# Down projection with five seven-product sets in every pair of column blocks, and weights loaded in half places

## The chip, the cores and the metric

The kernel runs on one core of a Trainium2 chip. The time is the device time of one execution in microseconds, the median of the runs. Five engines work side by side and meet only at semaphores: TensorE (PE) multiplies, VectorE (DVE) and ScalarE (ACT) work elementwise, GpSimd (POOL) here mostly issues accumulating DMAs, SyncE (SP) issues the loads.

## The reference

Two layers over 256 tokens of 2048 features. Layer 0 mixes by causal pooling, layer 1 by windowed attention; each is followed by a gated feed-forward part of 5632 columns. A change in the last product of that part is what this case is about:

```python
D_MODEL = 2048; SEQ = 256; DEPTH = 2
D_FF = ((8 * D_MODEL // 3 + 255) // 256) * 256          # 5632

def swiglu(x, wg, wu, wd):
    return (jax.nn.silu(x @ wg) * (x @ wu)) @ wd

for layer in range(DEPTH):
    ...                                                  # pooling mixer, or K/V, Q and attention
    h = h + swiglu(rmsnorm(h, ffn_norm[layer]), w_gate[layer], w_up[layer], w_down[layer])
return rmsnorm(h, final_norm)
```

All of it is float32, and the output is the whole (1, 256, 2048) array.

## The kernel before

**Precision.** Every float32 factor is split in two parts that TensorE can take in its faster format: `w_hi` is a rounded copy of the weights, made by ScalarE, and `w_lo` what is left, made by VectorE as `raw - w_hi`. A product is then three matmuls of 128 by 128 by 512: hi by hi, hi by `w_lo`, lo by hi.

**Units.** Weights pass through a ring of four places (`RING = 4`). A unit is 128 x 1024 weights, two tiles of 128 rows by 512 columns. For unit n ScalarE waits until TensorE has used unit n-4 and until the raw weights have landed, and rounds (L924 in the down projection, `L690` with a gain in K/V and Q); VectorE subtracts (L1538; L1129 in K/V and Q) and raises `unit_ready`; TensorE multiplies and raises `unit_used`. All three walk the same list of units in order, and everything else that ScalarE and VectorE do is hung behind a unit of that list.

**The down projection** of a layer (`down(l)` on each engine, planned by `DownPlan`) multiplies the 256 x 5632 matrix hT with w_down, 44 row tiles by four column blocks of 512. Blocks are done in two pairs (0 and 1, then 2 and 3). An **own** unit is two row tiles of one block for both token tiles: 12 matmuls. A **set** replaces eight own half products by seven: four row tiles of both blocks of a pair are taken as a 2 x 2 matrix B11, B12, B21, B22 of 256 x 512 each and multiplied with sums of quarters of hT in seven units B11, B21, B22, T1, T2, T3, T4 of 6 matmuls each. Four row tiles of a pair thus cost 42 matmuls in 7 units as a set and 48 in 4 units as own. The order is written out by hand in `DOWN_ORDER`, one character a unit: 0 and 1 are own units of the pair's first and second block, a, b, c are B11, B21, B22, and t, u, v, w are T1 to T4. `DOWN_SETS = [(4, 3), (4, 4)]` says how many sets the pairs of layer 0 and of layer 1 have: 15 in all, 109 units in layer 0 and 112 in layer 1.

**The sums of a set.** T1 is B11 with B12 added, T2 is T1 with B22 added, T4 is B21 with T2 added, T3 is B22 with B12 added (signs are carried by the other factor). Before, a set has two whole places of 1024 KB, loaded from column blocks one and two. GpSimd adds B12 to B11 by an SBUF-to-SBUF accumulating DMA (L2235, waited for as `d1_in`), waits for it, and adds B22 onto B12 in the same way (L2237, `d3_in`). T2 and T4 are added by VectorE (L1546, L1550) behind fixed units. The other factor's sums, "rows", are made per set by VectorE (`down_sums`, L1474 to L1482, and L1486) and ScalarE (L946).

**Loads.** SyncE issues 44 loads of 1024 KB a layer (L630), each when the unit that used its place last has been split.

**Around the matmuls.** At the start of `down` the last turn of the gate and up products is still being finished: `gate_add`, `sum_silu`, `up_add`, `common_out`, two whole transposes of 128 x 512 on VectorE (`quad_turn`, L1294) and, on ScalarE, sixteen copies of 32 x 256 (`quad_move`, L729) that put the 32 x 32 blocks in their places. When a pair's last set is done, `pair_common` adds the shared sums into h; when a block's last unit is done, `down_out` adds the block's products (L1216). In layer 0, blocks 0 to 2 of h are then transposed for the K/V and Q products that follow, on VectorE, as 16 transposes of 32 x 256 per block that write straight into place (`h_turn`, L1192, in four steps of four), rounded by ScalarE (`x_hi_part`, L714) and subtracted by VectorE (`x_lo_part`, L1199). Block 3 is transposed by TensorE inside K/V. ScalarE also sums squares of each block (L761). In the last four units of layer 1 TensorE does token tile 0 first and then tile 1 in two halves, so that the final norm can start (`finish`).

The positions of these steps come from formulas and small lists (`SET_AT`, `UP_AT`, `QUAD_AT`, `LAST_AT`, `down_turn`, `out_after`).

Of the kernel before, what the change touches and what calls it, by code (L numbers as in the profile page):

```python
# [26 lines left out]
F32 = mybir.dt.float32  # L27
# [5 lines left out]
P = 128  # L33
# [79 lines left out]
class TurnsPlan:  # L113

    def __init__(self):
# [8 lines left out]
        self.count = [0] * HALVES  # L124
# [15 lines left out]
FIRST_SLOT = ("B11", "B21", "T1", "T2", "T4")  # L140
HALF = {"B11": 0, "B21": 2 * C, "T1": 0, "T2": 0, "T3": 0, "T4": 2 * C, "B22": 2 * C}
DOWN_SETS = [(4, 3), (4, 4)]


DOWN_ORDER = [('a000b00t000acu1wb1tvcubwav11001100cat0ucb0wtvuvw11111111',
               '00a0000bc00taubvc0t01u1vwba1cw001tu1wv000101111111111'),
              ('0a01b1t00uwvca0001b0c01t0avuc1wbt111uw110ac0b00t1vuwv111',
               'b00a00act0b0utwvbacuw0v000001a1btcuwc1t1uvwv101011111111')]


@dataclass
class Load:

    slot: int
    block: int
    k0: int
    nth: int
    ready: int
    first: int
# [3 lines left out]
class Unit:  # L163
# [6 lines left out]
    load: Load  # L170
    second: object
    off: int
# [4 lines left out]
class DownPlan:  # L177

    def __init__(self, sets, order):
        self.units, self.loads = [], []  # L180
# [16 lines left out]
        needs = {}  # L197
        for n, (pair, form, n_set, m, k) in enumerate(where):
            if form == "own":
                needs.setdefault((pair, "own", m, k // 4 * 4), []).append(n)  # L200
                continue
            if form in FIRST_SLOT:
                needs.setdefault((pair, "sum", 0, 4 * n_set), []).append(n)
            if form not in ("B11", "B21", "T4"):
                needs.setdefault((pair, "sum", 1, 4 * n_set), []).append(n)
        self.free = [max(TURNS.free[2 * i:2 * i + 2]) - SUM_STEPS for i in range(SLOTS)]
        rows_used = max(AT[u] for u in SUM_ORDER if u[0] in PARTS) + 1
        self.free[RING] = max(self.free[RING], rows_used + RING - SUM_UNITS)
        count = [0] * SLOTS
        loads = {}  # L210
        for key in sorted(needs, key=lambda key: (needs[key][0], key[2])):
            pair, kind, m, k = key
            slot = min(range(SLOTS), key=lambda one: (self.free[one], one))
            count[slot] += 1
            loads[key] = Load(slot, 2 * pair + m, k, count[slot], self.free[slot], needs[key][0])
            self.loads.append(loads[key])
            self.free[slot] = max(needs[key]) + 1
        self.loads.sort(key=lambda one: (one.ready, one.first, one.slot))
        self.count = count

        self.sums = {}
        for pair, form, n_set in sorted((one for one in self.at if one[1] == "T1"), key=self.at.get):
            n = self.at[pair, form, n_set]
            self.sums.setdefault(n, []).append((pair, "T2", n_set))
            self.sums.setdefault(min(n + 1, self.at[pair, "T4", n_set] - 1), []).append((pair, "T4", n_set))
        self.nth_sum = {one: n for n, one in enumerate(one for n in sorted(self.sums) for one in self.sums[n])}
        self.set_order = sorted((one[::2] for one in self.at if one[1] == "B11"),
                                key=lambda one: self.at[one[0], "B11", one[1]])
# [13 lines left out]
        for n, (pair, form, n_set, m, k) in enumerate(where):  # L242
            if form == "own":
                load, second, off = loads[pair, "own", m, k // 4 * 4], None, k % 4 * C
            else:
                off = HALF[form]
                load = loads[pair, "sum", 0 if form in FIRST_SLOT else 1, 4 * n_set]
                second = loads[pair, "sum", 1, 4 * n_set]
            self.units.append(Unit(pair, form, n_set, m, k, load, second, off,
                                   tuple(opened[d] == n for d in banks[n]), tuple(closed[d] == n for d in banks[n])))  # L250

DOWN = [DownPlan(DOWN_SETS[l], DOWN_ORDER[l]) for l in range(2)]
# [3 lines left out]
class Lap:  # L256
# [17 lines left out]
    def loads(self, slot):  # L274
        more = -2 * SUM_TURNS * self.layers + (DOWN[0].count[slot] - 4 * UF // 8) * self.downs
        return self.n + more
# [39 lines left out]
def trunk(nc, x, pool_w, pool_rows, pool_scale, w_kv, w_q, w_o, w_gate, w_up, w_down, final_norm,  # L316
# [6 lines left out]
    down_v = [rows(w_down[l]) for l in range(2)]  # L323
# [5 lines left out]
    with ExitStack() as ctx:  # L329
# [38 lines left out]
        last_quad = [at(f"last_quad{l}", [P, T, C], F32, o_xhi + 4 * (0, 12)[l] * S) for l in range(2)]  # L368
        def d_home(l, n):
            tile = D_TILE[l][n]  # L370
            return (o_s1hi, o_s1lo) if tile is None else (o_xhi + 4 * tile * S, o_xlo + 4 * tile * S)
# [67 lines left out]
        raw_in = [sem(f"raw_in{i}") for i in range(RING + 1)]  # L439
        half_in = [sem(f"half_in{i}") for i in range(HALVES)]  # L440
# [99 lines left out]
        def out_after(l, b):  # L540
            plan = DOWN[l]
# [1784 lines left out]
```

## Time and profile before

| | |
|---|---|
| median of 3 runs | 1644.01 us (1641.56 to 1646.27) |
| profiled execution | 1647.76 us, span of its trace 1646.0 us |
| PE busy | 1630.0 us, 99% of the span |
| VectorE, ScalarE, GpSimd busy | 1441.4, 1196.3, 162.9 us |
| down projection, layer 0 | 494.9 to 724.9 us |
| down projection, layer 1 | about 1405 to 1639 us, the final norm behind it |
| granted TensorE clock | 0.999 of full speed |

A table of stretches gives, for each engine, its busy time and the number of its instructions in the stretch, then the granted clock and the busy share of the DMA engines. A timeline row gives the start, the length, engine, line, operation, what is written and read, how many instructions are merged, and in brackets how long the engine stood idle before it and what ended that. The length of an instruction in a row can overlap the next one's start: in a dense stretch the distance between starts is what an instruction costs. Times are us from the start of the span.

### The profile page before, as it was taken

The numbers are of one execution on the slowest core, as the hardware profiler recorded it, in microseconds if no ns is written. First come the engines' busy times: TensorE is split into PE (matmuls) and PEld (weight loads), VectorE is DVE, ScalarE is ACT, GpSimd is POOL, SyncE is SP. The second block draws the span as 40 slices with busy tenths as digits, with TensorE's granted clock in tenths as the row PEclk, the third lists the DMA queues.
The fourth block names the chain that finished last, engine by engine and source line by source line (L and its number), as shares of the span: only waits on it lengthen the run. The fifth ranks groups of instructions, "written<-read, shape, count | busy, mean of one in ns | idle before, by whom it ended". The sixth has DMA issues, their size and how long they took to land.

```text
span 1646.0 us, 20218 instructions
## 1 busy us (share of the span) xinstructions
PE 1630.0 (99%) x7396; PEld 1339.1 (81%) x7396; DVE 1441.4 (88%) x1622; ACT 1196.3 (73%) x1720; POOL 162.9 (10%) x204
## 2 busy tenths in 40 slices
PE   9999999999999999999999999999999999999998
PEld 8888888888888888888777888888887888788887
DVE  6899999999999898777676869999999999888867
ACT  6688888888867755556665567888888887676653
POOL 1111111111100000002010001111111111000000
PEclk9999999999999999999999999999999999999999
DMA  8578888888888887855444556888888888887783
GB/s 297 187 187 251 243 246 244 246 244 245 245 225 232 236 269 211 262 179 191 142 130 153 183 215 160 236 241 242 242 247 241 237 243 233 279 236 248 217 260 143
DMA packets 136571, 368.98 MB, mean 224 GB/s; under 512 B 9876, under 2 KB 10004, under 8 KB 136344
## 3 DMA queue, kind: packets, MB, share of 16 engines
q1 hardware_dynamic: 114576, 298.46, 51.1%
q0 software_dynamic: 21600, 68.17, 23.0%
q8 instruction: 59, 0.97, 0.2%
q10 hardware_dynamic: 296, 1.06, 0.2%
q14 instruction: 40, 0.33, 0.1%
HBM read 349.82 MB, written 2.10 MB: 214 GB/s over the span
## 4 chain that ended last, share of the span: by engine, by line
PE 82%; DMA 8%; DVE 6%; ACT 2%; issue 1%; SPq 0%; ACTq 0%; POOLq 0%
PE acc L1926 7%; PE acc L1928 7%; PE acc L1927 7%; PE acc L1775 6%; PE acc L1776 6%; PE acc L1777 6%; PE acc L2018 5%; PE acc L2020 5%; PE acc L2019 5%; DMA raw<-w_up_in 5%; PE acc L1903 5%; PE acc L1905 5%; PE acc L1907 5%; PE acc L2003 3%; PE acc L2004 3%; PE acc L2005 3%
## 5 line engine op out<-in xcount | busy, mean ns | idle before, releaser
L843 ACT ACTIVATE w_hi<-raw 128x1024 fp32r<-128x1024 f32 (+1 forms) x500 | 490.2, 1005 | 109.6 <-PE acc L1907 53.8
L1375 DVE TENSOR_TENSOR w_lo<-raw,w_hi 128x1024 fp32r<-128x1024 f32 (+1 forms) x460 | 507.4, 1149 | 17.0 <-ACT w_hi L843 14.9
L924 ACT ACTIVATE w_hi<-raw 128x1024 fp32r<-128x1024 f32 x221 | 232.8, 1060 | 160.3 <-PE acc L2020 112.6
L1538 DVE TENSOR_TENSOR w_lo<-raw,w_hi 128x1024 fp32r<-128x1024 f32 x221 | 265.9, 1222 | 62.4 <-ACT w_hi L924 57.3
L2224 POOL DMA_DIRECT2D raw<-w_up_in x120 | 104.6, 872 | 833.7 <-DVE w_lo L1372 504.5
L1903 PE MATMUL acc<-w_hi,xT_hi 128*128 128x512 f32 x480 | 186.8, 389 | 0.0
L1905 PE MATMUL acc<-w_lo,xT_hi 128*128 128x512 f32 x480 | 186.8, 389 | 0.0
L1907 PE MATMUL acc<-w_hi,xT_lo 128*128 128x512 f32 x480 | 186.7, 389 | 0.0
L2018 PE MATMUL acc<-w_hi,hT_hi 128*128 128x512 f32 x456 | 177.7, 390 | 1.6 <-DVE w_lo L1538 1.3
L2020 PE MATMUL acc<-w_hi,hT_lo 128*128 128x512 f32 x456 | 177.4, 389 | 0.0
L2019 PE MATMUL acc<-w_lo,hT_hi 128*128 128x512 f32 x456 | 177.4, 389 | 0.0
L729 ACT ACTIVATE hT_f<-quad 32x256 f32<-32x256 f32 x320 | 132.8, 415 | 4.5
L1926 PE MATMUL acc<-w_hi,s_hi 128*128 128x512 f32 x320 | 125.9, 393 | 3.2 <-DVE w_lo L1375 3.1
L1928 PE MATMUL acc<-w_hi,s_lo 128*128 128x512 f32 x320 | 124.7, 390 | 0.0
L1927 PE MATMUL acc<-w_lo,s_hi 128*128 128x512 f32 x320 | 124.6, 389 | 0.0
L1124 DVE TENSOR_TENSOR w_lo<-raw,w_hi 128x1024 fp32r<-128x1024 f32 x72 | 88.2, 1236 | 31.9 <-ACT w_hi L687 31.6
L687 ACT ACTIVATE w_hi<-raw 128x1024 fp32r<-128x1024 f32 x72 | 75.5, 1063 | 54.3 <-PE acc L1777 48.9
L1775 PE MATMUL acc<-w_hi,xT_hi 128*128 128x512 f32 x288 | 114.2, 397 | 0.0
L1777 PE MATMUL acc<-w_hi,xT_lo 128*128 128x512 f32 x288 | 112.2, 390 | 0.0
L1776 PE MATMUL acc<-w_lo,xT_hi 128*128 128x512 f32 x288 | 112.1, 389 | 0.0
L1926 PE MATMUL acc<-w_hi,xT_hi 128*128 128x512 f32 x280 | 109.0, 389 | 0.0
L1928 PE MATMUL acc<-w_hi,xT_lo 128*128 128x512 f32 x280 | 109.0, 389 | 0.0
(222 smaller groups left out, 3087.2 us busy)
## 6 DMA issues: line engine op xcount, KB each, us to landing
raw<-w_down_in SPq DMA_DIRECT2D x88, 1024.0 KB, 6.7
raw<-w_gate_in SPq DMA_DIRECT2D x160, 512.0 KB, 6.1
raw<-w_up_in SPq DMA_DIRECT2D x100, 512.0 KB, 6.1
raw<-w_up_in POOLq DMA_DIRECT2D x80, 512.0 KB, 7.5
raw<-w_q_in SPq DMA_DIRECT2D x16, 1024.0 KB, 5.1
raw<-w_o_in SPq DMA_DIRECT2D x16, 1024.0 KB, 5.1
raw<-raw POOLq DMA_DIRECT2D x30, 512.0 KB, 5.9
raw<-w_up_in POOLq DMA_DIRECT2D x40, 256.0 KB, 5.5
```

What stands on the lines that cost most here:

```text
L843: nc.scalar.activation(w_hi[:, (before + n) % RING, 0:src.shape[-1]], src, ACT.Copy, scale=-1.0 if form == "B11" else 1.0).then_inc(hi_rea ...
L1375: nc.vector.tensor_tensor(lo, src, hi, ALU.subtract).then_inc(unit_ready, 1)
L1538: nc.vector.tensor_tensor(w_lo[:, LAP_DOWN[l].ring(n), :], src, w_hi[:, LAP_DOWN[l].ring(n), :].bitcast(F32), ALU.subtract).then_inc(unit_ ...
L1903: nc.tensor.matmul(dst, xT_hi[:, k, tok], w_hi[:, w, cols], start=start, stop=False, skip_group_check=True)
L1905: nc.tensor.matmul(dst, xT_hi[:, k, tok], w_lo[:, w, cols], start=False, stop=False, skip_group_check=True)
L1907: last = nc.tensor.matmul(dst, xT_lo[:, k, tok], w_hi[:, w, cols], start=False, stop=stop, skip_group_check=True)
L1926: nc.tensor.matmul(dst, x_hi, w_hi[:, w, cols], start=start, stop=False, skip_group_check=True)
L1927: nc.tensor.matmul(dst, x_hi, w_lo[:, w, cols], start=False, stop=False, skip_group_check=True)
L1928: last = nc.tensor.matmul(dst, x_lo, w_hi[:, w, cols], start=False, stop=stop, skip_group_check=True)
L2018: nc.tensor.matmul(dst, hT_hi[:, k, tok], w_hi[:, LAP_DOWN[l].ring(n), cols], start=start, stop=False)
L2019: nc.tensor.matmul(dst, hT_hi[:, k, tok], w_lo[:, LAP_DOWN[l].ring(n), cols], start=False, stop=False)
L2020: last = nc.tensor.matmul(dst, hT_lo[:, k, tok], w_hi[:, LAP_DOWN[l].ring(n), cols], start=False, stop=stop)
```

## The change

1. `DOWN_SETS` becomes `[(5, 5), (5, 5)]`: 20 sets, 118 units in each layer, with new orders. All four pairs now have 24 own units and 35 of sets.
2. Weights are loaded in half places of 512 KB, one unit each (78 loads a layer), from a w_down that is laid out by blocks outside the kernel, so that a partition's part is one run of 4 KB and not four of 2 KB. B12 is no longer loaded: GpSimd adds it twice from DRAM, onto B11 (T1) and, after the T2 sum, onto B22 (T3). These 20 DMAs a layer go by `accums`, sorted by place, with at most four under way (`DOWN_LANES`).
3. In layer 0, h is transposed by two whole 128 x 512 transposes per block on VectorE into `h_quad`, and ScalarE moves the blocks by 16 copies of 32 x 256 per block (`h_move`).
4. Every step beside the matmuls gets a place of its own in `DOWN_AT`.
5. In `pair_common` VectorE waits for ScalarE's copy before its first add and not after it.

```diff
-DOWN_SETS = [(4, 3), (4, 4)]
+DOWN_SETS = [(5, 5), (5, 5)]
-DOWN_ORDER = [('a000b00t000acu1wb1tvcubwav11001100cat0ucb0wtvuvw11111111',
-               '00a0000bc00taubvc0t01u1vwba1cw001tu1wv000101111111111'),
...
+DOWN_ORDER = [('baab000101c01b10c1t0auw1tav10t1wa1vcub01ct0tcwbvuuvuwwv1001',
+               'aa0cbaa011ttbcuwcatwcuuvt1vtc0bv0vu0uv10b1w1bww010000101111'),
+              ('ba0b01001a100at10cwu10at1cvuca1tw10ut1vcut0cbvuvwb1bwvw0101',
+               'aaa000c0bctccw1au0t1ut0vbawb1v0wut0ct1buv10wvbuwv1101001111')]
+DOWN_AT = [{...
+     "copy": (57, 109), "common": (57, 108), "out": (61, 61, 115), "squares": (87, 105, 117),
+     "h_turn": ((98, 102), (97, 100), (115, 115)),
+     "h_moves": ((103, 105, 108, 110, 110, 113, 113, 114), (102, 108, 108, 111, 111, 113, 113, 115), (117, 117, 117, 117, 117, 117, 117, 117)),
+     "x_hi": (115, 117, 117), "x_lo": (117, 117, 117)},
...
+            def h_move(b, n):
+
+                if n == 0:
+                    ac.wait_ge(h_turned, T * (b + 1))
+                pb = n // 2
+                for q in (2 * (n % 2), 2 * (n % 2) + 1):
+                    src = h_quad[b][pb * QUAD:(pb + 1) * QUAD, :, :].rearrange("c t (k q r) -> c k t q r", k=4, q=4)
+                    dst = xT_f[q * QUAD:(q + 1) * QUAD, 4 * b:4 * b + 4, :].rearrange(
+                        "c k (t b r) -> c k t b r", t=T, b=4)
+                    last = nc.scalar.activation(dst[:, :, :, pb, :], src[:, :, :, q, :], ACT.Copy)
+                if n == 7:
+                    last.then_inc(xt_full, 1)
...
+                    if form == "own":
+                        src = down_v[l][2 * pair + m, k // 2]
+                    else:
+                        src = down_v[l][2 * pair + (form == "B22"), 2 * m + (form != "B11")]
+                    sp.dma_start(down_half(one), src.rearrange("p k n -> p (k n)")).then_inc(half_in[one.half], 16)
...
-                    gp.dma_start(first[:, 0:2 * C], second[:, 0:2 * C], accum_op=ALU.add).then_inc(d1_in, 16)
-                    gp.wait_ge(d1_in, 16 * (c + 1))
-                    gp.dma_start(second[:, 0:2 * C], second[:, 2 * C:], accum_op=ALU.add).then_inc(d3_in[c % 2], 16)
+                    base = {"T1": "B11", "T3": "B22"}[form]
+                    gp.wait_ge(unit_ready, before + plan.at[pair, base, n_set] + 1)
+                    if form == "T3":
+                        gp.wait_ge(d_sum, down_sum(l, (pair, "T2", n_set)))
+                    if c >= DOWN_LANES:
+                        gp.wait_ge(*lane(c - DOWN_LANES))
+                    b12 = down_v[l][2 * pair + 1, 2 * n_set].rearrange("p k n -> p (k n)")
+                    gp.dma_start(set_half(l, pair, base, n_set), b12, accum_op=ALU.add).then_inc(lane(c)[0], 16)
```

Two places as the engines' programs show them. First, ScalarE at the end of layer 0's down projection and the start of K/V, before. `w_hi` from `raw` is the rounding of a unit (the last four are own units), `unused,sumsq<-h` the squares of block 2, `xT_hi<-xT_f` the rounding of its transposed block, `w_hi<-raw,gains` half of a K/V unit.

```order
L761 ACTIVATE unused_113,sumsq_119<-h_49 128x2x2x128 [waits sq_done,job_out,pair_step]
L761 ACTIVATE unused_113,sumsq_119<-h_49 128x2x2x128 [waits sq_done]
L924 ACTIVATE w_hi_60<-raw_59 128x1024 [waits unit_used]
L924 ACTIVATE w_hi_60<-raw_59 128x1024 [waits raw_in0,unit_used]
L924 ACTIVATE w_hi_60<-raw_59 128x1024 [waits unit_used]
L924 ACTIVATE w_hi_60<-raw_59 128x1024 [waits raw_in2,unit_used]
L714 ACTIVATE xT_hi_56<-xT_f_58 128x1024 [waits xt_full]
L924 ACTIVATE w_hi_60<-raw_59 128x1024 [waits unit_used]
L690 ACTIVATE w_hi_60<-raw_59,gains_115 128x512 [waits unit_used,raw_in0]
L690 ACTIVATE w_hi_60<-raw_59,gains_115 128x512
```

And the same place after, where `h_quad2` is the transposed block 2:

```order
L929 ACTIVATE w_hi_60<-raw_59 128x1024 [waits half_in2,unit_used]
L929 ACTIVATE w_hi_60<-raw_59 128x1024 [waits half_in6,unit_used]
L772 ACTIVATE unused_124,sumsq_130<-h_49 128x2x2x128 [waits sq_done,job_out,pair_step]
L772 ACTIVATE unused_124,sumsq_130<-h_49 128x2x2x128 [waits sq_done]
L712 ACTIVATE xT_hi_56<-xT_f_58 128x1024 [waits xt_full]
L740 ACTIVATE xT_f_58<-h_quad2_82 32x8x32 [waits h_turned]
L740 ACTIVATE xT_f_58<-h_quad2_82 32x8x32 x15
L712 ACTIVATE xT_hi_56<-xT_f_58 128x1024 [waits xt_full]
L688 ACTIVATE w_hi_60<-raw_59,gains_126 128x512 [waits unit_used,raw_in0]
L688 ACTIVATE w_hi_60<-raw_59,gains_126 128x512
```

The squares of block 2 stood five units before the end; now they, two roundings of transposed blocks and all sixteen moves of block 2 stand between the rounding of the last down unit and that of the first K/V unit.

Second, VectorE at the same place, before: the last steps of `h_turn` for block 2, three splits, the subtraction, and the first K/V split.

```order
L1192 STREAM_TRANSPOSE xT_f<-h 32x2x4x32 x4
L1538 TENSOR_TENSOR w_lo<-raw,w_hi 128x1024 [waits hi_ready]
L1192 STREAM_TRANSPOSE xT_f<-h 32x2x4x32 x4
L1538 TENSOR_TENSOR w_lo<-raw,w_hi 128x1024 [waits hi_ready] x3
L1199 TENSOR_TENSOR xT_lo<-xT_f,xT_hi 128x1024 [waits xt_hi]
L1129 SCALAR_TENSOR_TENSOR w_lo<-raw,gains,w_hi 128x512 [waits hi_ready]
```

And after, from `down_out` of block 2 on:

```order
L1228 SCALAR_TENSOR_TENSOR h<-acc,r,h 128x512 [waits unit_used,pair_step]
L1228 SCALAR_TENSOR_TENSOR h<-acc,r,h 128x512
L1596 STREAM_TRANSPOSE h_quad_82<-h 128x512 [waits unit_used,pair_step,job_out]
L1596 STREAM_TRANSPOSE h_quad_82<-h 128x512
L1549 TENSOR_TENSOR w_lo<-raw,w_hi 128x1024 [waits hi_ready] x2
L1211 TENSOR_TENSOR xT_lo<-xT_f,xT_hi 128x1024 [waits xt_hi] x3
L1141 SCALAR_TENSOR_TENSOR w_lo<-raw,gains,w_hi 128x512 [waits hi_ready]
```

`down_out` of block 2 stood behind unit 101 of 0 to 108; now it stands behind unit 115 of 0 to 117, and three subtractions of transposed blocks stand ahead of the first K/V split.

## Rows read from the trace of the kernel before

**Rows 1.** Stretches of both down projections: us; PE, PEld, DVE, ACT, POOL busy; clock; DMA

```profile
494.90:724.90 230.00, 229.74 (x1012) 189.48 (x1011) 202.95 (x224) 143.55 (x169) 12.15 (x14) 1.00 0.75 230
1404.60:1632.20 227.60, 225.91 (x995) 186.03 (x994) 187.02 (x179) 142.22 (x166) 13.90 (x16) 1.00 0.77 232
```

**Rows 2.** TensorE's waits: who waited, for whom, us in total, times, longest

```profile
PE acc L1810 <- DVE hT_lo L1136: 1.8, 1, 1.8
...
PE acc L2018 <- DVE w_lo L1538: 1.3, 2, 1.1
```

**Rows 3.** Timeline of TensorE, layer 0: an own unit, then a set's unit (first matmuls)

```profile
576.75 0.39 PE L2018 MATMUL acc<-w_hi,hT_hi 128*128 128x512 f32 x1
...
579.47 0.39 PE L2003 MATMUL acc<-w_hi,hT_hi 128*128 128x512 f32 x1
...
580.83 0.39 PE L2003 MATMUL acc<-w_hi,d_hi 128*128 128x512 f32 x1
```

**Rows 4.** Groups on VectorE, layer 0's down projection: busy us, mean ns | idle before

```profile
L1538 DVE TENSOR_TENSOR w_lo<-raw,w_hi 128x1024 fp32r<-128x1024 f32 x108 | 129.8, 1222 | 22.2 <-ACT w_hi L924 19.4
L1192 DVE STREAM_TRANSPOSE xT_f<-h 32x256 f32<-32x256 f32 x48 | 20.9, 436 | 0.8
L1546 DVE TENSOR_TENSOR raw<-raw 128x1024 f32<-128x1024 f32 x7 | 8.5, 1219 | 0.0
```

**Rows 5.** The same table for ScalarE: the copies that move turned blocks

```profile
L729 ACT ACTIVATE hT_f<-last_quad 32x256 f32<-32x256 f32 x16 | 6.6, 415 | 0.3
```

**Rows 6.** Timeline of VectorE: a split, a whole transpose, a split; and a `down_out`

```profile
504.28 1.22 DVE L1538 TENSOR_TENSOR w_lo<-raw,w_hi 128x1024 fp32r<-128x1024 f32 x1
505.42 0.70 DVE L1294 STREAM_TRANSPOSE last_quad<-act 128x512 f32<-128x512 f32 x1
506.04 1.18 DVE L1538 TENSOR_TENSOR w_lo<-raw,w_hi 128x1024 fp32r<-128x1024 f32 x1
...
1619.18 1.40 DVE L1216 SCALAR_TENSOR_TENSOR h<-acc,r,h 128x512 f32<-128x512 f32 x2
```

**Rows 7.** Timeline of ScalarE: two copies, and the squares of one block

```profile
508.42 0.85 ACT L729 ACTIVATE hT_f<-quad 32x256 f32<-32x256 f32 x2
...
702.53 0.61 ACT L761 ACTIVATE unused<-h 128x512 f32<-128x512 f32 x1
...
703.26 0.63 ACT L761 ACTIVATE unused<-h 128x512 f32<-128x512 f32 x1
```

**Rows 8.** Timeline of ScalarE where layer 0's down projection ends

```profile
713.41 1.04 ACT L714 ACTIVATE xT_hi<-xT_f 128x1024 fp32r<-128x1024 f32 x1
715.16 1.06 ACT L924 ACTIVATE w_hi<-raw 128x1024 fp32r<-128x1024 f32 x1 [0.71 <-PE acc L2020]
719.15 2.79 ACT L690 ACTIVATE w_hi<-raw,gains 128x512 fp32r<-128x512 f32 x4 [2.93 <-DMA raw<-w_kv_in]
```

**Rows 9.** Timeline of VectorE at the same place: the first two K/V units

```profile
720.52 2.87 DVE L1129 SCALAR_TENSOR_TENSOR w_lo<-raw,gains,w_hi 128x512 fp32r<-128x512 f32 x4 [1.91 <-ACT w_hi L690]
```

**Rows 10.** The chain in order of time, where layer 1's down projection waits

```profile
1410.86 8.01 DMA raw<-raw
...
1424.20 0.50 PE acc L2018
...
1543.18 8.37 DMA raw<-w_down_in
```

**Rows 11.** DMA issues of the whole run: count, KB each, median us to landing

```profile
raw<-w_down_in SPq DMA_DIRECT2D x88, 1024.0 KB, 6.7
...
raw<-w_up_in SPq DMA_DIRECT2D x100, 512.0 KB, 6.1
raw<-w_up_in POOLq DMA_DIRECT2D x80, 512.0 KB, 7.5
```

**Rows 12.** From issue to landing of the 512 KB loads of L624: least, median, most

```profile
DMA to landing us min/median/max: 2.5/6.2/11.1
```

**Rows 13.** A stretch around TensorE's longest wait, columns as in the first group

```profile
24.00:32.00 8.00, 6.24 (x35) 5.19 (x34) 7.53 (x12) 5.48 (x10) 2.05 (x2) 1.00 0.81 295
```

**Rows 14.** Timeline of VectorE at the end: the wait for the last matmuls

```profile
1639.01 0.48 DVE L1731 SCALAR_TENSOR_TENSOR hblk<-acc,r,hblk 128x256 f32<-128x256 f32 x1 [0.89 <-PE acc L2177]
```

More of the change, by code:

```diff
@@ L169 @@
     k0: int
-    load: Load
-    second: object
-    off: int
+    piece: Piece
     opens: tuple
@@ L218, in __init__ @@
[L218 to L226, printed above, removed]
@@ L227, in __init__ @@
-        self.set_order = sorted((one[::2] for one in self.at if one[1] == "B11"),
-                                key=lambda one: self.at[one[0], "B11", one[1]])
+        self.sums = {}
+        for pair in range(2):
+            for m in range(sets[pair]):
+                n = self.at[pair, "T1", m]
+                self.sums.setdefault(n, []).append((pair, "T2", m))
+                n = max(min(n + 1, self.at[pair, "T4", m] - 1), self.at[pair, "B21", m])
+                self.sums.setdefault(n, []).append((pair, "T4", m))
@@ new lines, in __init__, with at @@
+        self.nth_sum = {one: n for n, one in enumerate(one for n in sorted(self.sums) for one in self.sums[n])}
+        sum_at = {one: n for n in self.sums for one in self.sums[n]}
+        life = {}
+        for n, (pair, form, m, block, k) in enumerate(where):
+            if form == "own":
+                life[pair, "own", block, k] = (n, n)
+        for pair in range(2):
+            for m in range(sets[pair]):
+                def at(form):
+                    return self.at[pair, form, m]
+                life[pair, "B11", m, 0] = (at("B11"), max(at("T2"), sum_at[pair, "T4", m] + 1))
+                life[pair, "B21", m, 0] = (at("B21"), at("T4"))
+                life[pair, "B22", m, 0] = (min(at("B22"), sum_at[pair, "T2", m]), at("T3"))
@@ L229, in __init__ @@
+        self.pieces.sort(key=lambda one: (one[0].ready, one[0].first, one[0].half))
+        self.accums = sorted([(self.at[p, "B11", m], 0, "T1", p, m) for p in range(2) for m in range(sets[p])]
+                             + [(max(self.at[p, "B22", m], sum_at[p, "T2", m]), 1, "T3", p, m)
+                                for p in range(2) for m in range(sets[p])])
+        self.nth_accum = {one[2:]: c for c, one in enumerate(self.accums)}
         opened, closed = {}, {}
@@ L242, in __init__ @@
         for n, (pair, form, n_set, m, k) in enumerate(where):
[L243 to L249, printed above, removed]
+            piece = self.of[pair, "own", m, k] if form == "own" else self.of[pair, PLACE[form], n_set, 0]
+            self.units.append(Unit(pair, form, n_set, m, k, piece,
                                    tuple(opened[d] == n for d in banks[n]), tuple(closed[d] == n for d in banks[n])))
+DOWN_LANES = 4
 DOWN = [DownPlan(DOWN_SETS[l], DOWN_ORDER[l]) for l in range(2)]
@@ L322, in trunk @@
     up_v = [w_up[l] for l in range(2)]
-    down_v = [rows(w_down[l]) for l in range(2)]
+    down_v = [w_down[l] for l in range(2)]
     kv_v, q_v, o_v = rows(w_kv), rows(w_q[0]), rows(w_o[0])
@@ L1587, in _ @@
+                    if l == 1:
+                        for b, when in enumerate(at["gain"]):
+                            if n == when:
+                                ve.wait_ge(pair_step, 8 * (2 + b // 2 + 1))
+                                final_gain(b)
             gate_up(0, 0, True)
```

282 lines of the change are left out of this document (129 added, 153 removed).

## The prediction

> **What bounds the kernel now.** I read the busy times by stretch first, then who waited for whom, then timelines. In both down projections TensorE is busy for all but 0.26 us and 1.69 us, at the full granted clock [rows 1], and over the whole run its listed waits are a few tenths to 1.8 us [rows 2]. The bound is the number of matmuls, so the first question is what a matmul costs: not the 0.39 us of its row, since rows overlap, but the distance between starts. An own unit of 12 matmuls runs from 576.75 to 579.47, that is 2.72 us or 0.227 us a matmul; a set's unit of six takes 1.36 us [rows 3]. The second question is whether the feeders keep up. VectorE is busy 203 of 230 us in layer 0's down projection and 187 of 227.6 us in layer 1's, ScalarE some 143 us in each [rows 1]. In a dense stretch a split costs VectorE 1.14 us (504.28 to 505.42) [rows 6], against 1.36 us for a set's unit on TensorE: only 0.22 us is over, and the ring is four units deep.
>
> **Matmuls removed.** A set saves 6 matmuls. Layer 0 goes from 7 sets to 10, layer 1 from 8 to 10: 18 + 12 = 30 matmuls. TensorE's programs differ by just that, so this step can't fail to happen. 30 x 0.227 = **-6.8 us** (4.1 and 2.7), on the engine that sets the end.
>
> **Splits and sums added.** Layer 0 gets 9 more units, 6 more T2 or T4 sums and one more set of rows. By [rows 4] that is 9 x 1.22 + 6 x 1.22 on VectorE, and for the rows some 4.1 us (two instructions of 1.22 and four of 0.42); the 48 small transposes (20.9 us) become six whole ones of 0.70 [rows 4, 6], 16.7 us less. VectorE goes from 203 to 209 of about 226 us. Layer 1 gets 6 units, 4 sums and a set of rows: 187 + 16.3 = 203 of 226 us. This all lies beside TensorE as long as no stretch asks more of VectorE than four units of lead can lend. I summed, place by place, VectorE's steps against TensorE's units in the new order: a set's unit lends 0.22 us, an own unit 1.58, a sum takes 1.14. The lead that a unit's split has on TensorE is then 0.4 us at the least (layer 0, unit 37, behind rows and a sum), mostly 0.7 to 3. So the cost is 0; if that cover is gone at the tightest places, some tenths each. ScalarE: 24 pairs of moves of 0.85 [rows 7] in layer 0, with 9 roundings: about 143 + 31 = 174 of 226 us. Room on the whole; where it is at the end is the next term.
>
> **The end of layer 0's down projection.** Here is what I expect to go wrong. Before, the last block's ten own units cover all the turning of block 2: its rounding is over at 714.4, the first K/V unit is rounded from 719.15, when its load lands, and TensorE does not wait [rows 8, 9]. After, block 2's last unit is 113, and only units 114 to 117 remain: 4 x 2.72 = 10.9 us of cover. Time from the end of unit 113: semaphore 0.3; `down_out` on VectorE 1.4 [rows 6], to 1.7; the squares on ScalarE 2 x 0.73 [rows 7], to 3.2; rounding block 1, 1.0 (1.04 in its row [rows 8]), to 4.2; sixteen moves at 0.425 [rows 5, 7], 6.8, to 11.0; rounding block 2, 1.0, to 12.0; the first K/V unit's rounding, two of four in 2.79, so 1.4 [rows 8], to 13.4; its split, two of four in 2.87 [rows 9], to 14.8. VectorE's two transposes end by 3.0 and bind nothing. TensorE runs out at 10.9: **+3.9 us** of wait, with nothing else for it to do, since it walks the list in order. Bounds: 3.4 if every step is at its row's distance with no semaphore delay, 4.5 with 0.1 us at each of the six handovers. Behind ScalarE's moves K/V's roundings are queued, behind VectorE's subtraction of block 2 K/V's splits; units 2 on have their lead back, since 1.4 us per unit is fed and 2.7 used. K/V's loads, now released by units 115 to 117, land inside this wait.
>
> **Waits that go.** Layer 1 waits 1.1 us at 1424.20, behind an SBUF-to-SBUF accumulate of 8.01 us [rows 10] whose B11 stood only five units ahead. In the new orders B11 stands at least 15 us ahead of its T1, and T2 and B22 at least 12 us ahead of T3; the slowest comparable accumulate, DRAM to SBUF, has a median of 7.5 us [rows 11]. So that wait goes: **-1.1**. Also -0.3, the wait behind the 8.37 us load at 1543 [rows 10], and -0.2 in layer 0, where the small transposes crowd VectorE. The 0.3 us of "issue" I leave.
>
> **Loads.** Bytes fall: a set moves 2.5 MB and not 3. What counts is the time between a place's release and its next use. Six places are close. Tightest: layer 1's unit 76, released by unit 72: TensorE's units 72 to 75 take 6.8 us, the split of 72 leads by 0.9, and rounding and split of 76 take 2.4: 5.3 us for a load whose like has a median of 6.2 and ranges from 2.5 to 11.1 [rows 12]. **+0.9**, bounds 0 and 5.8. Next: layer 0's unit 30 (6.4 us), 79 (7.3), layer 1's 86, 87, 89 (7.3, 7.4, 7.8): 0 at the median. Before, the tightest were 8.0 and 8.1 for 1024 KB loads of 6.7 [rows 11], and one gave the 0.3 us.
>
> What rows show of size: 512 KB loads land in 6.1 us, 1024 KB in 6.7 [rows 11], so halves land sooner but not in half the time. The Trainium skill's "DMA: Bandwidth & Descriptors", section "Measured (HBM→SBUF, 128 partitions, SWDGE, issued from GpSimd)", speaks against the change: batch DMAs to 1 MiB or more for at least 75% of peak. By that rule the halves would be slow and the late-load case below the likely one; by the rows, the sum stands.
>
> **The end of the kernel.** Before, the second tile's last part waits 0.89 us for TensorE [rows 14]. After, block 2's add, two splits, and two gains stand in the last four units. The split of unit 116 is ready 0.2 us after TensorE wants it: **+0.2**. `finish` of tile 0 starts 0.6 us later than it could, inside the 0.89. The changed order of copy and add in `pair_common` has 8 us of own units above it: 0.
>
> **Sum.** -6.8 + 3.9 - 1.6 + 0.9 + 0.2 = **-3.4 us**. The profiled execution took 1647.76 us, 3.75 above the median: it would become 1644.4. The median becomes 1644.0 - 3.4 = **1640.6 us**. A measurement of this kernel tells about 0.3%, 4.9 us, from no change.
>
> **Rivals.**
> 1. The end of layer 0 is covered after all, say because moves beside an idle list run closer: 3.9 falls away, **1636.7**. For: the steps are many and I sum them singly. Against: each is a row, and ScalarE does them in order. 0.12.
> 2. VectorE does not keep up. At 92% busy, ten sums of 20 stand within a set-heavy run; 0.3 us at each of ten places is 3.0: **1643.6**. For: before, it waited only 22.2 us for roundings in that stretch [rows 4]. Against: the summed lead never falls below 0.4. 0.13.
> 3. Slower: late loads. If the halves land in 8.4 us, like the load in [rows 10], the six places above miss by 2.0 + 1.1 + 3.1 + 1.1 + 1.0 + 0.6 = 8.9 us, 8.0 more than I count: **1648.6**. From 7.5 us of landing on it eats the gain (3.8 - 0.9 = 2.9). For: the accumulates from DRAM now come by 20 a layer with up to four under way. Against: fewer bytes. 0.13.
> 4. The wait breaks TensorE's clock. Rows show waits up to 1.8 us with the clock still at the higher of its levels, 2.4 GHz, in the stretch around [rows 2, 13]; 3.9 us is not shown. At 1.2 GHz a matmul takes 0.227 us more. For as long as the wait itself, that is 1.9 us, **1642.5**; for all 96 matmuls of K/V 21.8 us, 1662.4. It outweighs the gain from 15 matmuls on. 0.10, of which a quarter beyond 1649.
>
> The Trainium skill's "TensorE: Matmul & The Clock Gate", section "What's actually happening", says that the throttled state is the default and activity releases it. By that, rival 4 would hold; no row here has a wait that long, so it stays a rival.
>
> **How the numbers follow.** Forecast 0.50, rivals 0.12, 0.13, 0.13, 0.10, other 0.02. The likeliest case alone: 1638.5 to 1642.5. The range of 1636.5 to 1647.5 takes in rivals 1 and 2 and most of 4, and half of 3. Faster by over 0.3% is below 1639.1: rival 1 and a quarter of the forecast (a run's spread), 0.25. Slower, above 1648.9: a little under half of 3, a quarter of 4 and the rest, 0.10. Within: 0.65.
>
> **What would show it.** Right: 996 matmuls in each down projection; one TensorE wait of 3.4 to 4.5 us at the first K/V unit, ended by VectorE's split and behind sixteen copies on ScalarE; no wait of T1 or T3 for an accumulate; about 1 us at unit 76 of layer 1 behind a load. VectorE at 209 and 203 us. Wrong: no wait at K/V, many waits of tenths in sets, a granted clock below full behind the K/V wait, or loads that land above 7.5 us.

## The result, and the profile after

| | before | after |
|---|---|---|
| median of 22 runs each | 1642.95 us (1640.48 to 1646.38) | 1645.95 us (1642.71 to 1648.13) |
| ratio to before | | 1.0019, 95% interval 1.0013 to 1.0025 |
| profiled execution, span | 1647.76 us, 1646.0 us | 1647.64 us, 1645.9 us |
| PE busy | 1630.0 us | 1625.7 us |

The changed kernel is slower by 0.19%, about 3.0 us, where I forecast 3.4 us less. The time lies inside the range and inside "within 0.3%"; the sign is wrong, and the sum is short by 6.4 us. (I forecast from a median of 3 runs, 1644.01 us; that of 22 is 1642.95, so the differences are what can be compared.) TensorE's busy time fell by 4.3 us, although some of its matmuls became slower: the gain was made and then given back, mostly as waits.

The two profiled executions happen to take the same time: that of before is 4.8 us above its median, that of after 1.7. Their totals can't be subtracted, so I compare stages. The first table of waits is TensorE's in the changed kernel (for whom, us in total, times, longest) and answers to [rows 2]:

```profile
PE acc L2037 <- DVE w_lo L1549: 4.2, 3, 2.8
PE acc L1794 <- DVE w_lo L1141: 3.8, 1, 3.8
PE acc L1829 <- DVE hT_lo L1148: 1.7, 1, 1.7
```

The K/V wait of 3.8 us is the one forecast. The 2.8 us in a down projection is new. The stages, from the starts of TensorE's first matmul in each (its timeline, in us from the span's start; in brackets the length of the stage):

| kernel | layer 0 down | K/V | layer 1 down | last matmul |
|---|---|---|---|---|
| before | 495.08 | 725.84 (230.76) | 1407.83 (681.99) | 1638.69 (230.86) |
| after | 495.92 | 731.47 (235.55) | 1411.24 (679.77) | 1638.90 (227.66) |

Layer 1 gained 3.2 us; layer 0 lost 4.8, and 1.8 more at the start of K/V. The stretch between, which the change touches only by those 1.8 us at its start, is 2.2 us shorter all the same. Over all profiles below it ranges from 678.2 to 683.0, well beyond those 1.8 us, so a difference of some two us in it is the spread of an execution.

TensorE's timeline in the changed kernel, at the two waits (start, length, line, in brackets the idle time before):

```profile
556.89 0.39 PE L2024 MATMUL acc<-w_hi,d_lo 128*128 128x512 f32 x1
560.04 0.50 PE L2037 MATMUL acc<-w_hi,hT_hi 128*128 128x512 f32 x1 [2.76 <-DVE w_lo L1549]
...
561.43 0.63 PE L2038 MATMUL acc<-w_lo,hT_hi 128*128 128x512 f32 x1
561.86 0.63 PE L2039 MATMUL acc<-w_hi,hT_lo 128*128 128x512 f32 x1
...
564.26 0.40 PE L2039 MATMUL acc<-w_hi,hT_lo 128*128 128x512 f32 x1
...
731.47 0.77 PE L1794 MATMUL acc<-w_hi,xT_hi 128*128 128x512 f32 x1 [3.78 <-DVE w_lo L1141]
...
734.89 0.40 PE L1796 MATMUL acc<-w_hi,xT_lo 128*128 128x512 f32 x1
```

Read the distances. After the wait a matmul starts 0.43 us after the one before it (561.43, 561.86), not 0.227 as in [rows 3]. From 560.04 to 564.26 eleven steps take 4.22 us and would take 2.49 at full speed: 1.73 us lost on top of the wait. At K/V the eight steps from 731.47 to 734.89 take 3.42 us for 1.81, which is 1.6 lost. A wait also delays the next start by 0.16 us more than its idle time in the row, since the last matmul's length overlaps; with that K/V's price behind its wait is 1.77. The stretches say why; columns as in [rows 1], with the granted clock third from the end:

```profile
555.00:560.00 5.00, 2.28 (x11) 1.54 (x9) 1.24 (x2) 2.28 (x4) 0.00 (x0) 1.00 0.49 193
560.00:564.00 4.00, 3.96 (x11) 3.12 (x12) 4.00 (x4) 3.38 (x5) 0.21 (x1) 0.58 0.61 157
564.00:568.00 4.00, 4.00 (x19) 3.30 (x18) 3.71 (x4) 2.68 (x3) 0.66 (x1) 0.99 0.82 187
...
731.00:735.00 4.00, 3.54 (x9) 2.85 (x10) 4.00 (x7) 2.55 (x5) 0.00 (x0) 0.57 0.28 46
```

The clock was granted at 0.58 and 0.57 in the four microseconds after each wait, most of which thus lie at the lower of its levels (1.2 GHz), and behind unit 30 it is back at 0.99, the higher one (2.4 GHz). So both waits cost about 1.8 us more than they last.

What ended the first? The chain in order of time, then ScalarE's timeline, then the DMA issues of 543 to 549 us (count, KB, median us to landing), all of the changed kernel:

```profile
548.47 9.12 DMA raw<-w_down_in
557.67 1.07 ACT w_hi L929
558.76 1.24 DVE w_lo L1549
560.04 0.50 PE acc L2037
```

```profile
557.67 1.06 ACT L929 ACTIVATE w_hi<-raw 128x1024 fp32r<-128x1024 f32 x1 [4.61 <-DMA raw<-w_down_in]
```

```profile
raw<-w_down_in POOLq DMA_DIRECT2D x2, 512.0 KB, 8.2
raw<-w_down_in SPq DMA_DIRECT2D x1, 512.0 KB, 9.1
```

This is layer 0's unit 30, one of the six places whose budget I had worked out (6.4 us), and its load took 9.1. After it landed came only its rounding (1.07 us) and its split (1.24), so nothing else held the unit back. GpSimd had started two accumulates just before it:

```profile
545.68 1.76 POOL L2256 DMA_DIRECT2D raw<-w_down_in  x2 [6.74 <-issue]
```

One more wait in layer 0 was not forecast: 0.86 us at 694.75, unit 106, with 0.1 to 0.2 us of slower matmuls behind it. In layer 1 there is one of 0.62 at 1574.33, unit 87, behind a load of 8.0 us.

### The profile page after: what moved, and what is told of

Same layout as the page of the kernel before. It is cut to its first block, busy times and chain, and to the rows that moved or that the text cites. A ratio compares the mean times of both kernels' runs of the same rounds, so it can differ in the third digit from the quotient of the medians.

```text
span 1645.9 us, 20453 instructions
## 1 busy us (share of the span) xinstructions
PE 1625.7 (99%) x7366; PEld 1336.3 (81%) x7366; DVE 1457.8 (89%) x1617; ACT 1233.2 (75%) x1785; POOL 171.6 (10%) x214
## 4 chain that ended last, share of the span: by engine, by line
PE 88%; DMA 4%; DVE 4%; ACT 2%; issue 1%; SPq 0%; ACTq 0%; POOLq 0%; DVEq 0%
PE acc L1945 8%; PE acc L1947 8%; PE acc L1946 8%; PE acc L1794 6%; PE acc L1922 6%; PE acc L1926 6%; PE acc L1924 6%; PE acc L1796 6%; PE acc L1795 6%; PE acc L2037 5%; PE acc L2039 5%; PE acc L2038 5%; PE acc L2023 3%; PE acc L2022 3%; PE acc L2024 3%; DMA raw<-w_up_in 2%
## 5 line engine op out<-in xcount | busy, mean ns | idle before, releaser
L929 ACT ACTIVATE w_hi<-raw 128x1024 fp32r<-128x1024 f32 x236 | 248.2, 1060 | 138.1 <-PE acc L2039 87.9
L1549 DVE TENSOR_TENSOR w_lo<-raw,w_hi 128x1024 fp32r<-128x1024 f32 x236 | 282.0, 1219 | 42.4 <-ACT w_hi L929 37.4
L2037 PE MATMUL acc<-w_hi,hT_hi 128*128 128x512 f32 x376 | 147.5, 392 | 4.2 <-DVE w_lo L1549 4.2
L2039 PE MATMUL acc<-w_hi,hT_lo 128*128 128x512 f32 x376 | 147.0, 391 | 0.0
L2038 PE MATMUL acc<-w_lo,hT_hi 128*128 128x512 f32 x376 | 146.9, 391 | 0.0
L1136 DVE TENSOR_TENSOR w_lo<-raw,w_hi 128x1024 fp32r<-128x1024 f32 x72 | 88.1, 1235 | 31.9 <-ACT w_hi L685 31.6
L685 ACT ACTIVATE w_hi<-raw 128x1024 fp32r<-128x1024 f32 x72 | 75.5, 1063 | 54.3 <-PE acc L1796 49.0
```

The lines of the kernel that those rows point to most:

```text
L929: nc.scalar.activation(w_hi[:, LAP_DOWN[l].ring(n), :], down_half(unit.piece), ACT.Copy).then_inc(hi_ready, 1)
L1549: nc.vector.tensor_tensor(w_lo[:, LAP_DOWN[l].ring(n), :], down_half(unit.piece), w_hi[:, LAP_DOWN[l].ring(n), :].bitcast(F32), ALU.subtra ...
L2037: nc.tensor.matmul(dst, hT_hi[:, k, tok], w_hi[:, LAP_DOWN[l].ring(n), cols], start=start, stop=False)
L2039: last = nc.tensor.matmul(dst, hT_lo[:, k, tok], w_hi[:, LAP_DOWN[l].ring(n), cols], start=False, stop=stop)
```

## The experiments

The theory: the gain from the matmuls, 6.8 us, is there in full; it is paid away by two waits on TensorE, each with a fall of the granted clock. Wait one is a load that shares the DMA engines with accumulates, wait two ScalarE's queue at the end of layer 0. Rivals: that load is slow by itself; the end is bound by another engine or by loads once ScalarE is relieved; the slow matmuls have a cause other than TensorE's idleness.

**The accumulate moved.** `down_turn_sums`, on GpSimd; set 3's B12 is needed at unit 41 and was added after unit 25:

```
+ late = 31 if (l, form, pair, n_set) == (0, "T1", 0, 3) else 0
- gp.wait_ge(unit_ready, before + plan.at[pair, base, n_set] + 1)
+ gp.wait_ge(unit_ready, before + max(plan.at[pair, base, n_set] + 1, late))
```

> The changed kernel with one edit: in layer 0 GpSimd starts the first accumulate of set 3 (pair 0) after the split of unit 30 instead of after that of unit 25; it is needed at unit 41. In the profile of the changed kernel this accumulate and another one started at 546.6 and 545.7 us, and the load for unit 30 that was issued at 548.5 us between them landed after 9.1 us against a budget of 6.4. Theory A (the load was late because it shared the DMA engines with two accumulates): the load lands within 7.5 us, the wait of 2.76 us at unit 30 is under 0.8, no matmul stretch there at 0.43 us spacing (those cost 1.73 us), and the time falls by 3 to 4.5 us against the changed kernel (ratio to the kernel before 1.0019 -> 0.9993 to 1.0001). Theory B (this load is slow by itself, or the wait happened in that one execution only): the landing stays at 8 to 9 us and the wait stays, or the time stays within 0.5 us of the changed kernel's.

Measured: 1643.26 us, ratio 0.9999 (0.9988 to 1.0009). GpSimd's timeline shows the second accumulate gone from beside the first, and the DMA issues of 544 to 548.5 us show what that does for the loads:

```profile
544.96 0.86 POOL L2257 DMA_DIRECT2D raw<-w_down_in  x1 [6.74 <-issue]
555.08 0.86 POOL L2257 DMA_DIRECT2D raw<-w_down_in  x1 [9.25 <-DVE w_lo L1549]
```

```profile
raw<-w_down_in POOLq DMA_DIRECT2D x1, 512.0 KB, 5.5
raw<-w_down_in SPq DMA_DIRECT2D x1, 512.0 KB, 4.0
```

Landing fell from 9.1 to 4.0 us, the wait at unit 30 is gone, no matmul near it stands at 0.43 us, and layer 0's stage is 231.70 instead of 235.55 us. Theory A holds. In the three kernels below that also keep the two accumulates together, the waits there were 1.92, 2.09 and 2.23 us, behind loads of 8.3, 8.4 and 8.6 us: it is a property of the kernel and not of one execution.

**K/V's first units ahead of block 2.** ScalarE's loop over the K/V units (VectorE's subtraction of block 2 follows its unit 3 likewise):

```
- for b in range(NBLK - 1):          # in down(0): h_moves, x_hi
+ for b in range(NBLK - 2):
...
  round_hi(LAP_KV, i, tiles, off, G_KV, k0)
+ if i in (1, 2):
+     for part in range(4 * i - 4, 4 * i):
+         h_move(2, part)
+ if i == 3:
+     x_hi_part(0, 2)
```

> The changed kernel with one edit at the end of layer 0: ScalarE rounds the first two K/V weight units before the 16 moves of block 2, the third between them and the fourth before block 2 is rounded; VectorE rounds block 2 after the fourth unit. TensorE needs block 2 only from the fifth K/V unit on. Theory A (the 3.78 us wait is ScalarE's 6.81 us of moves standing ahead of the first K/V unit in its queue, and the clock then costs 1.77 us more): no wait over 0.3 us at the start of K/V, none over 0.5 us at the fifth unit, full-speed spacing of 0.227 us throughout, time 5 to 5.5 us below the changed kernel's (ratio to before about 0.9987). Theory B (VectorE's chain or the K/V loads would come next): a wait of 1 to 3 us remains at the start or at the fifth unit, and the gain is under 3 us.

Measured: 1640.31 us, ratio 0.9985 (0.9975 to 0.9995). ScalarE's timeline, where K/V now starts at 724.97 without a wait:

```profile
718.19 1.32 ACT L688 ACTIVATE w_hi<-raw,gains 128x512 fp32r<-128x512 f32 x2
719.73 1.34 ACT L688 ACTIVATE w_hi<-raw,gains 128x512 fp32r<-128x512 f32 x2 [0.22 <-PE acc L2046]
720.98 3.39 ACT L740 ACTIVATE xT_f<-h_quad 32x256 f32<-32x256 f32 x8
724.38 1.34 ACT L688 ACTIVATE w_hi<-raw,gains 128x512 fp32r<-128x512 f32 x2
725.74 3.40 ACT L740 ACTIVATE xT_f<-h_quad 32x256 f32<-32x256 f32 x8
```

The same 16 moves, 6.8 us, are there; eight now stand behind the roundings of two K/V units and eight behind those of three. K/V's first four units read blocks 0 and 1 alone. Nothing came next: no wait at the fifth unit, clock 1.00. Theory A holds.

**Both.** The two edits in one kernel, run twice, the second time beside the kernels that are compared with it.

> Both edits (late accumulate of set 3, K/V units ahead of block 2's moves). If the two waits and the clock after each are the whole of what the forecast missed (2.76 + 1.73 + 3.78 + 1.77 = 10.0 us), the time is about 1636 us where the kernel before has 1643, ratio 0.9955 to 0.9970. If the clock falls or waits come for another reason, the ratio stays over 0.998.

> The kernel with both edits once more, on the chip of the next three, as what they are compared with. Both theories expect the ratio of the earlier run within its interval (0.9949 to 0.9973).

Measured: 1635.51 us, ratio 0.9961 (0.9949 to 0.9973), and again 1635.35 us, 0.9954 (0.9939 to 0.9969). This version beats both kernels: 7 us or 0.4% below before, some 10 below the changed kernel. Its two down projections, columns and stretches as in [rows 1]:

```profile
492.00:719.50 227.50, 226.44 (x997) 186.70 (x996) 204.14 (x203) 168.38 (x217) 16.55 (x19) 1.00 0.74 217
1399.00:1626.00 227.00, 226.60 (x1020) 187.88 (x1019) 204.21 (x206) 149.71 (x174) 16.57 (x19) 1.00 0.74 211
```

TensorE idles 1.1 and 0.4 us, with VectorE at 204 of 227 us in both. The two waits with what follows them, 10.1 us, account for the whole distance to the changed kernel, to within the interval of about 2 us either way.

**TensorE kept at work in the K/V wait.** Ahead of the first K/V unit:

```
+ if u == 0:
+     for _ in range(14):
+         nc.tensor.matmul(pair_bank(JOB_KV % 2, 0), xT_hi[:, 0, 0:P], xT_hi[:, 0:2, :],
+                          start=True, stop=True)
```

> The changed kernel with 14 matmuls of 512 columns, whose result the first K/V matmul overwrites, issued in the wait before the first K/V unit (14 x 0.227 = 3.2 us of the 3.78 us wait). The wait's end, set by ScalarE and VectorE, does not move. Theory A (the granted clock falls because TensorE stands idle there): the first K/V matmuls follow each other at 0.227 us, the granted clock of the stretch stays at 1.00, and the time falls by 1.5 to 1.8 us (ratio to before about 1.0008). Theory B (the slow matmuls after the wait have another cause, such as a shared SBUF port or the power of the other engines): the spacing of 0.43 us stays and the time is the changed kernel's within 0.5 us.

Measured: 1643.01 us, ratio 1.0008 (0.9998 to 1.0019), on theory A's value by its middle, but with an interval that reaches to theory B's. The timeline decides:

```profile
722.92 3.33 PE L2058 MATMUL acc<-xT_hi 128*128 128x512 f32 x14
726.78 0.50 PE L1794 MATMUL acc<-w_hi,xT_hi 128*128 128x512 f32 x1 [0.52 <-DVE w_lo L1141]
727.11 0.39 PE L1795 MATMUL acc<-w_lo,xT_hi 128*128 128x512 f32 x1
727.34 0.40 PE L1796 MATMUL acc<-w_hi,xT_lo 128*128 128x512 f32 x1
```

K/V starts as late as before against the end of the down projection, with ScalarE and VectorE doing the same; its matmuls stand at 0.33 us once and then at 0.23. Only TensorE's idle time was changed, and the slow stretch is gone: the clock fell because TensorE stood idle, and matmuls for nothing save that part of the cost.

**Half as many of them.** 7 instead of 14.

> The changed kernel with 7 instead of 14 idle-time matmuls before the first K/V unit, so that TensorE works for 1.6 us of the 3.78 us and then stands for 2.2. Idle stretches of 1.92, 2.23, 2.76 and 3.78 us were each followed by a fall of the granted clock that cost 1.77 to 1.87 us; one of 2.12 us (in the kernel with small transposes) by none (0.48 us). Theory A (a stand of this length is enough, whatever came before it): the matmuls after it stand at 0.43 us again and the time is the changed kernel's within 0.5 us. Theory B (it is not the length alone): the clock stays at 1.00 there and the time falls by about 1.3 to 1.6 us against the changed kernel's ratio of 1.0019.

Measured: 1643.36 us, ratio 1.0009 (1.0000 to 1.0019). One profile holds both outcomes; TensorE's timeline, then the clock of the stretches behind the waits:

```profile
555.13 0.79 PE L2037 MATMUL acc<-w_hi,hT_hi 128*128 128x512 f32 x1 [2.09 <-DVE w_lo L1549]
555.72 0.63 PE L2038 MATMUL acc<-w_lo,hT_hi 128*128 128x512 f32 x1
...
726.43 0.50 PE L1794 MATMUL acc<-w_hi,xT_hi 128*128 128x512 f32 x1 [2.10 <-DVE w_lo L1141]
726.77 0.40 PE L1795 MATMUL acc<-w_lo,xT_hi 128*128 128x512 f32 x1
```

```profile
555.00:559.00 4.00, 3.87 (x10) 3.11 (x11) 4.00 (x5) 3.47 (x5) 0.11 (x1) 0.57 0.55 167
726.40:730.40 4.00, 3.96 (x17) 3.30 (x18) 4.00 (x7) 3.07 (x6) 0.00 (x0) 1.00 0.34 68
```

After 2.09 us of standing the clock fell, after 2.10 us it did not. So the length of one wait does not decide alone. What does is open: the waits after which it fell all stand at unit 30 or are the full 3.78 us, and nothing here varied the one without the other. Nor does the fall stand at the wait itself: in the kernel with 14 idle-time matmuls, four matmuls behind the wait of 2.23 us at unit 30 still take 1.05 us together, and only then come those at 0.42 to 0.43 us.

**Copies for accumulates.** This kernel leaves the sums with B12 out of layer 0's down projection; it tells only of time.

```
- gp.dma_start(set_half(...), b12, accum_op=ALU.add)
+ gp.dma_start(set_half(...), b12)                    # layer 0 only
```

> The changed kernel, but in layer 0's down projection each of GpSimd's 20 transfers of B12 copies the half-size piece over the place instead of accumulating on it; the sum with B11 or B22 is left out of the computation there, so the run tells only of time. Bytes read from DRAM, sizes and moments of issue stay. Theory A (the accumulates are what slows the neighbouring loads, by more than their bytes): these transfers land within 5 to 6.5 us instead of 5.6 and 10.8, the load for unit 30 within 7.5 us instead of 9.1, the wait there is under 1 us and the time falls by 3 to 4.5 us against the changed kernel (ratio 0.9992 to 1.0001). Theory B (three transfers of 512 KB that start within 3 us are late whatever they do with their bytes): landing of 8.5 us or more, the wait of 1.9 to 2.8 us and the ratio of 1.0019 stay.

Measured: 1642.46 us, ratio 0.9993 (0.9984 to 1.0001), with no wait at unit 30. The DMA issues of layer 0's down projection in the changed kernel:

```profile
raw<-w_down_in SPq DMA_DIRECT2D x68, 512.0 KB, 5.2
raw<-w_down_in POOLq DMA_DIRECT2D x20, 512.0 KB, 6.7
```

and with copies, at the same places with the same bytes from DRAM:

```profile
raw<-w_down_in SPq DMA_DIRECT2D x68, 512.0 KB, 4.6
raw<-w_down_in POOLq DMA_DIRECT2D x20, 512.0 KB, 4.4
```

The transfers themselves land 2.3 us sooner and the neighbouring loads 0.6 us at the median, 2.8 at the worst (6.4 instead of 9.2). The load for unit 30 landed in 4.5 us beside two copies. Theory A holds: an accumulate costs its neighbours more than its bytes from DRAM. (It also works on what is in SBUF; whether that is the reason is not shown.)

**h turned as before.** From the kernel with both edits: `h_turn` on VectorE, 16 small transposes a block, at units 98, 100, 102, 106 and 107, 112 to 114, block 2 between the first K/V splits; no moves on ScalarE.

> The kernel with both edits, but h is turned as in the kernel before: VectorE writes all three blocks with 48 small transposes in place (16 a block at about 0.445 us each), ScalarE makes none of the 48 moves; block 2 is turned between VectorE's first K/V units. Per block VectorE spends 7.1 us instead of 1.3 and ScalarE 6.8 us less. Theory A (ScalarE had the slack to take the moves and VectorE had none near the end of pair 1, so whole transposes carry the sets): waits of 2 to 6 us in sum appear between units 98 and 117 of layer 0 or at the first K/V units, time 2 to 7 us above the kernel with both edits. Theory B (VectorE, idle for 7 of the last 30 us of the stage, holds the small transposes as well once block 2 may follow the first K/V units): no wait over 0.5 us there and the time within 1 us of the kernel with both edits.

Measured: 1641.42 us, ratio 0.9988 (0.9978 to 0.9997), 6 us above the kernel with both edits. VectorE's timeline at K/V:

```profile
724.34 1.42 DVE L1140 SCALAR_TENSOR_TENSOR w_lo<-raw,gains,w_hi 128x512 fp32r<-128x512 f32 x2
725.79 3.58 DVE L1203 STREAM_TRANSPOSE xT_f<-h 32x256 f32<-32x256 f32 x8
729.38 1.42 DVE L1140 SCALAR_TENSOR_TENSOR w_lo<-raw,gains,w_hi 128x512 fp32r<-128x512 f32 x2
```

TensorE waits 2.12 us at 730.94 for that split, 0.54 us in pair 1 with 0.7 behind it, and some tenths. With what follows them that is 4.0 us in its profile, but the kernel with both edits has 1.0 us at the same place in pair 1. So about 3 of the 6 us are placed and about 3 are not; whether they are spread between executions is not shown. Another placing of the transposes might do better. As placed here, theory A holds: the whole transposes and ScalarE's moves are worth their place.

**The rest of the waits.** Block 1's squares from unit 105 to 117 in layer 0, and in layer 1 set 3's accumulate later (79 for 75); then the squares alone:

```
- "squares": (87, 105, 117)
+ "squares": (87, 117, 117)
```

> The kernel with both edits, and two more of the same kind: in layer 1 the first accumulate of pair 1's set 3 starts after the split of unit 78 instead of after that of unit 74 (it is needed at unit 92), and in layer 0 the squares of block 1 move on ScalarE from unit 105 to unit 117. They aim at the two waits left in the down projections: 0.4 to 0.6 us at layer 1's unit 76, whose load landed after 8.0 us while two accumulates were under way, and 0.86 us in layer 0 (694.75 in the profile of the changed kernel), which the rows put behind 1.46 us of squares between two set units. If each wait goes with the 0.2 us that the next matmuls lose, the time falls by 1.5 to 1.9 us against the kernel with both edits. If the squares only push the K/V start (they then stand ahead of the first K/V weights on ScalarE), a wait of about 1 us appears there and the gain is under 0.8 us.

> The kernel with both edits and the squares of block 1 at unit 117 of layer 0 instead of unit 105, without the edit in layer 1 that the kernel with all waits also had. In that kernel the wait of 0.86 us at unit 106 was gone (layer 0's down projection took 226.1 us instead of 227.2) and two waits of 0.98 and 1.14 us were new in layer 1. Theory A (the new waits came from the accumulate that was moved in layer 1): layer 0's stage takes 226.1 us again, layer 1's 226.7 to 227.1 us, time about 1.1 us below the kernel with both edits (ratio to before 0.9945 to 0.9955). Theory B (the waits in layer 1 come and go by themselves between executions): a wait of about 1 us or more stands in layer 1's pair 1 again.

Measured: 1635.74 us, ratio 0.9955 (0.9942 to 0.9968), and 1635.97 us, 0.9960 (0.9947 to 0.9974): no gain that can be seen over the kernel with both edits, where the first text expected 1.5 to 1.9 us and theory A of the second 1.1. In both, layer 0's stage took 226.1 and 226.3 us instead of 227.2 and the wait of 0.86 us is gone, with none new at K/V. Layer 1's took 229.0 and 228.2 instead of 226.7: waits (which the first text wrongly puts at unit 76) at units 86 and 87 of 0.98 and 1.14 us, and of 0.74 and 0.62. I had picked the wrong accumulate (that of set 3 starts 12 us ahead of the slow load; set 2's second one is beside it), and GpSimd takes them in order, so the moved one held back the next:

```profile
1545.30 1.79 POOL L2264 DMA_DIRECT2D raw<-w_down_in  x2 [13.64 <-DVE w_lo L1554]
```

But the kernel without that edit has such waits too, so theory A of the second text fails and what is left speaks for B: at units 86 and 87 the waits range from none to 1.4 us in sum over the other profiles. What the edit in layer 1 costs by itself stays open.

## Why the prediction was wrong, step by step

Two steps failed. The load for layer 0's unit 30 was taken to land within its budget of 6.4 us; it took 9.1 and cost 2.8 us of wait and 1.8 of slow clock. The wait at K/V was forecast, and the fall of the clock behind it was left out of the sum: 1.8 us. A third term, ScalarE in pair 1, was put at nothing and cost 1.1.

- **Matmuls removed, -6.8: right.** No run varies this term alone, but the stages bear it out. In the first profile of the kernel with both edits layer 0's stage is 3.3 us shorter than before (230.76 - 227.50), for 4.1 + 0.2 less 1.1 at unit 106, and layer 1's 3.9 (230.86 - 227.00), for 2.7 + 1.1 + 0.3 less some 0.4 at unit 87. The medians say the same, 6.8 and 6.9 us below before (1642.35 - 1635.51 and 1642.27 - 1635.35), with an interval of some 2 us; that the number equals the term is chance, since it holds waits that went and one that came.
- **Splits and sums added, 0: nearly.** VectorE is at 204 us in either layer for 209 and 203 forecast, and in layer 0 no wait of more than 0.2 us lies with it: the 0.86 us (1.1 with what follows) comes from ScalarE, whose squares and moves stand between the roundings of two units there. I had summed VectorE place by place and ScalarE only on the whole.
- **The end of layer 0's down projection, +3.9: right in size, short in its price.** The wait was 3.78 us, behind sixteen moves, as worked out. But 1.77 us of slow clock followed. I had that as rival 4 with 0.10, and gave it 1.9 us at the wait's length. That this came so near is luck: the price does not follow the length, since shorter waits at unit 30 were followed by 1.7 to 1.8 us too. A slow matmul costs 0.2 us more (0.43 for 0.227), a little less than the 0.227 I took. The step that failed is leaving the clock out of the sum because no row showed a longer wait: [rows 13] speaks for waits up to 1.8 us only. Here the Trainium skill's "TensorE: Matmul & The Clock Gate", section "What's actually happening", pointed the right way: it says that the throttled state is the default and that activity releases it. The granted clock, 0.57 to 0.58 after both waits and at its full level again some four microseconds on, agrees.
- **Waits that go, -1.6: right.** Neither the wait for an accumulate nor that of 0.3 us at 1554 is in layer 1's stage any more.
- **Loads, +0.9: the step that failed.** I compared each budget with the median of landings over the whole run (6.2, and 5.4 measured for these) and called 6.4 us at unit 30 enough. The load there took 9.1, for 2.76 us of wait and 1.8 of clock. The median of a run says nothing of a load issued 2 to 3 us after two accumulates; the order says which those are, and I had it. Rival 3 had the mechanism ("up to four under way") but spread it over six places at 8.4 us, 8.0 us in all. At unit 76, my tightest, nothing happened; 0.62 us stood at unit 87, so the 0.9 in the sum came near the 0.75 measured at another place, by luck.
- **The end of the kernel, +0.2: nil.** The wait of [rows 14] is 0.73 us now instead of 0.89.

In sum: -3.4 + 2.8 + 1.8 (unit 30) + 1.8 (clock at K/V) + 1.1 (unit 106) = +4.1, less 0.1 for K/V's shorter wait and 0.2 for the kernel's end: +3.8, for +3.0 measured (interval 2.1 to 4.1).

The rule of "DMA: Bandwidth & Descriptors" in the Trainium skill, section "Measured (HBM→SBUF, 128 partitions, SWDGE, issued from GpSimd)", spoke for slow halves. By bytes for each microsecond of one load the trace agrees: 512 KB in 5.4 us at the median is 95 KB a microsecond, and the 1024 KB of before in 6.7 [rows 11] is 153. What the kernel waits for is the landing, and that comes sooner. The halves were late, at 9.1 and 8.0 us, where accumulates had started just before. No run here tests halves against whole places by themselves.

## What to carry to other kernels

Where a load is released late, hold its budget against what shares the DMA engines at that moment, not against the run's median; an accumulate started nearby counts for more than its bytes, and may often start later. At the end of a stage ask what its successor needs first, and queue on each engine only that ahead of it. A wait on TensorE of about 2 us or more may cost another 1.6 to 1.8 us in clock, as seven waits of 1.9 to 3.8 us here did and two of 2.1 did not, so price it with that, and if it can't be removed, fill it.

## What the runs showed of the hardware that I had not expected

- Idle stretches of TensorE of 1.92, 2.09, 2.23, 2.76 and 3.78 us were each followed by some four microseconds mostly at the lower clock level, 1.6 to 1.8 us lost from the first start on, whatever their length. Behind stretches of 2.10 us (after seven idle-time matmuls) and 2.12 us only 0.1 us was lost. The kernel before had none over 1.8 us.
- 512 KB from DRAM to SBUF on GpSimd's queue lands in 4.4 us as a copy and in 6.7 as an accumulate; the 512 KB load of unit 30 took 8.3 to 9.1 us beside two accumulates (four profiles), 4.0 beside one, 4.5 beside two copies.
